# Moving a residual from GpSimd to VectorE slices, and reordering four places around the output projections

## The reference

```python
for i in range(2):
    x = layer_norm(ALPHA * x + 0.5 * swiglu(x, ffn1_w_gate[i], ffn1_w_up[i], ffn1_w_down[i]), ln_g[i, 0], ln_b[i, 0])
    proj = x @ (rwkv_w_in if i == 0 else sb_w_in)
    mix = rwkv7_mix(...) if i == 0 else stick_breaking_mix(...)
    heads = concatenate([mix, memory_attention(mq, mem_k, mem_v)])
    x = layer_norm(ALPHA * x + heads @ w_out[i], ln_g[i, 1], ln_b[i, 1])
    x = layer_norm(ALPHA * x + 0.5 * swiglu(x, ffn2_w_gate[i], ffn2_w_up[i], ffn2_w_down[i]), ln_g[i, 2], ln_b[i, 2])
```

## Time and profile before

| | |
|---|---|
| median of 3 runs | 1634.25 us (1630.9 to 1635.93) |
| the profiled execution | 1636.34 us |
| its span, first to last instruction | 1634.6 us |
| TensorE busy, mean granted clock | 1460.2 us (89%), 0.942 |
| VectorE / ScalarE / GpSimd busy | 958.9 / 675.2 / 231.0 us |
| DMA moved | 257.71 MB, mean 158 GB/s |

### The profile page before, as it was taken

One profiled execution on the slowest core, in us unless ns is written; L12 is line 12 of the kernel. 1 busy time (PEld: TensorE's weight loads), 2 busy tenths in 40 slices (PEclk: granted clock), 3 DMA queues, 4 the chain that ended last, 5 costly groups with the idle time before them and its releaser, 6 DMA issues. The chain is left out here.

```text
span 1634.6 us, 30766 instructions
## 1 busy us (share of the span) xinstructions
PE 1460.2 (89%) x12484; PEld 1328.6 (81%) x12484; DVE 958.9 (59%) x1213; ACT 675.2 (41%) x848; POOL 231.0 (14%) x208
## 2 busy tenths in 40 slices
PE   5999799997999978939867999979999895799997
PEld 4777699996999968828856999969999794589997
DVE  2665576666555565674538555585555547475556
ACT  4445455444333345542324333343334445343332
POOL 1440132220000024002303000030000302030000
PEclk8999999998999989969978999989999897789999
DMA  9954466663666644300024666656665440366662
GB/s 362 345 178 186 129 204 190 190 181 106 192 192 180 181 137 143 114 1 4 4 77 130 193 185 187 180 149 185 182 191 168 155 155 1 103 202 180 182 188 95
DMA packets 297827, 257.71 MB, mean 158 GB/s; under 512 B 6928, under 2 KB 274192, under 8 KB 294672
## 3 DMA queue, kind: packets, MB, share of 16 engines
q1 hardware_dynamic: 297744, 256.49, 50.7%
HBM read 255.42 MB, written 1.05 MB: 157 GB/s over the span
## 5 line engine op out<-in xcount | busy, mean ns | idle before, releaser
L137 PE MATMUL ps<-actT,a_parts 128*128 128x256 f32 x2176 | 626.3, 288 | 22.0 <-DVE actT L399 10.4
L138 PE MATMUL ps<-actT,a_parts 128*128 128x256 f32 x2176 | 622.5, 286 | 0.0
L139 PE MATMUL ps<-actT,a_parts 128*128 128x256 f32 x2176 | 622.2, 286 | 0.0
L137 PEld LDWEIGHTS ps<-actT,a_parts 128*128 128x128 f32 x2176 | 424.4, 195 | 33.4 <-issue 18.4
L138 PEld LDWEIGHTS ps<-actT,a_parts 128*128 128x128 f32 x2176 | 424.6, 195 | 3.6
L139 PEld LDWEIGHTS ps<-actT,a_parts 128*128 128x128 f32 x2176 | 424.4, 195 | 0.0
L1111 DVE TENSOR_TENSOR a_parts<-a_raw,a_parts 128x2048 fp32r<-128x2048 f32 x100 | 239.7, 2397 | 72.9 <-ACT a_parts L1108 72.7
L1108 ACT ACTIVATE a_parts<-a_raw 128x2048 fp32r<-128x2048 f32 x100 | 190.0, 1900 | 0.0
L1125 DVE TENSOR_TENSOR b_parts<-b_raw,b_parts 128x1024 fp32r<-128x1024 f32 x72 | 88.3, 1226 | 154.3 <-ACT b_parts L1122 154.3
L1122 ACT ACTIVATE b_parts<-b_raw 128x1024 fp32r<-128x1024 f32 x90 | 95.1, 1057 | 175.8 <-PE ps L139 175.8
L137 PE MATMUL ps<-b_parts,hid 128*128 128x512 f32 x400 | 157.8, 394 | 6.3 <-DVE hid L1192 6.3
(11 more groups left out here) (343 smaller groups left out, 1801.0 us busy)
## 6 DMA issues: line engine op xcount, KB each, us to landing
a_raw<-in_ffn_w_gate SPq DMA_DIRECT2D x88, 512.0 KB, 3.9
a_raw<-in_ffn_w_up SPq DMA_DIRECT2D x88, 512.0 KB, 5.1
b_raw<-in_ffn_w_down SPq DMA_DIRECT2D x88, 512.0 KB, 3.2
arena<-in_mod_w SPq DMA_DIRECT2D x24, 1024.0 KB, 8.9
a_raw<-in_f_up_w SPq DMA_DIRECT2D x44, 512.0 KB, 4.9
b_raw<-in_f_down_w SPq DMA_DIRECT2D x22, 512.0 KB, 3.2
a_raw<-in_rwkv_w_in SPq DMA_DIRECT2D x10, 1024.0 KB, 5.2
a_raw<-in_sb_w_in SPq DMA_DIRECT2D x10, 1024.0 KB, 5.4
```

Source lines behind the costliest of these rows:

```text
L137: pe.matmul(out, lhs[0], rhs[0], start=start, stop=False)
L138: pe.matmul(out, lhs[0], rhs[1], start=False, stop=False)
L139: return pe.matmul(out, lhs[1], rhs[0], start=False, stop=stop)
```

## The change

- GpSimd's residual is gone. In the feed-forward stages with a residual, VectorE does it inside the loop: nine iterations, each with one slice of 114 columns of both token halves, multiplied between the two halves of the iteration and added at its end. `x_tok` and `rows` are two columns wider for this (9 x 114 = 1026).
- For the rwkv and stick stages the residual moves behind them, into the output projection: VectorE does half 0 before the split of chunk 2 and half 1 before that of chunk 3, four passes of 1024 columns in all; SyncE loads the two rows there ahead of the chunks.
- Output projection on TensorE: chunk 2 for three blocks, then chunk 3 for these, then the last block, with half 0 turned in between. Before: block by block, both chunks each.
- rwkv: the small weights are loaded behind chunk 4 instead of ahead of everything.
- First block: the parameter table is loaded in two parts; chunk 1 of the second pointwise product (`g_pw2 + 1`) is split earlier on ScalarE and VectorE.
- Convolutional feed-forward: the split of the next stage's first chunk moves behind the first half's update.

```diff
+             ("mod_sh_m", D, mod(0)), ("mod_sc_m", D, mod(1)),
              ("norm_pre_ffn", D, whole("norm_pre_ffn")), ("a_pw1_b", 2 * D, whole("a_pw1_b")),
              ("a_dw_b", D, whole("a_dw_b")), ("a_ln_g", D, whole("a_ln_g")), ("a_ln_b", D, whole("a_ln_b")),
-             ("mod_sh_m", D, mod(0)), ("mod_sc_m", D, mod(1)), ("mod_sh_f", D, mod(3)), ("mod_sc_f", D, mod(4)),
...
-        x_tok = sb("x_tok", [P, NT, D])
+        x_all = sb("x_tok", [P, NT, D + 2])
+        x_tok = x_all[:, :, 0:D]
...
-        rows = sb("rows", [P, 2, D])
+        rows_all = sb("rows", [P, 2, D + 2])
+        rows = rows_all[:, :, 0:D]
...
-        def residual(pool, i, scale_row, offset_row):
-
-            pool.wait_ge(token_turned[1], 2 * i + 2)
-            for t in range(NT):
-                pool_steps.step(pool, pool.tensor_tensor(x_tok[:, t], x_tok[:, t], scale_row, ALU.mult))
-                ins = pool.tensor_tensor(x_tok[:, t], x_tok[:, t], offset_row, ALU.add)
-            ins.then_inc(pool_out.up("xs"), 1)
...
-                    sp.dma_start(x_tok[:], A["x"][0].rearrange("(t p) d -> p t d", p=P)).then_inc(x_loaded, 16)
-                    sp.dma_start(par[:], A["par"]).then_inc(params_loaded, 16)
+                    sp.dma_start(x_tok, A["x"][0].rearrange("(t p) d -> p t d", p=P)).then_inc(x_loaded, 16)
+                    sp.dma_start(par[:, 0:n_first], A["par"][:, 0:n_first]).then_inc(params_loaded, 16)
...
                     ring_a.load(sp, g_pw1 + 1)
+                    sp.dma_start(par[:, n_first:], A["par"][:, n_first:]).then_inc(rest_loaded, 16)
...
+                        if q == 2:
+                            ring_a.split_hi(act, g_pw2 + 1)
...
-                    for c in range(1, 4):
+                    for c in range(2, 4):
...
+                    ring_a.split_lo(dve, g_pw2 + 1)
...
+        RES_STEP = 114
...
-                        sp.wait_ge(pool_out.sem, pool_out.at("xs"))
+                        sp.wait_ge(res_done, r0 + BODY - 2)
...
-                        if got_norm is not None:
-                            pool.wait_ge(rows_loaded, rows_at)
-                            residual(pool, got, rows[:, 0], rows[:, 1])
...
+                    def residual(op, slot, j):
+                        w = bass.ds(j * RES_STEP + -RES_STEP, RES_STEP)
+                        row = rows_all[:, slot, w].unsqueeze(1).to_broadcast([P, NT, RES_STEP])
+                        return dve.tensor_tensor(x_all[:, :, w], x_all[:, :, w], row, op)
+
                     def tiles_dve(j):
                         split_a(None, dve, 0, j)
                         tile_dve(dve, 1, j - 1)
                         if not conv:
                             split_b(None, dve, 0, j)
+                        if got_norm is not None:
+                            residual(ALU.mult, 0, j).then_inc(res_scaled, 1)
                         split_a(None, dve, 1, j)
                         tile_dve(dve, 0, j)
                         if not conv:
                             split_b(None, dve, 1, j)
-
+                        if got_norm is not None:
+                            dve.wait_ge(res_scaled, j + r0)
+                            residual(ALU.add, 1, j).then_inc(res_done, 1)
+
+                    if got_norm is not None:
+                        dve.wait_ge(rows_loaded, rows_at)
                     with dve.Fori(1, BODY - 1) as j:
                         tiles_dve(j)
                     split_a(None, dve, 0, BODY - 1)
...
-                        ring_a.split_lo(dve, next_a)
-                    if conv:
...
                         updated(0)
+                        ring_a.split_lo(dve, next_a)
                         gated_y(1)
                         updated(1)
...
+                    load_row(sp, 0, norm_row("g", got_norm))
+                    load_row(sp, 1, norm_row("b", got_norm))
                     for g in range(g0 + 2, g0 + 4 + 2):
                         ring_a.load(sp, g)
...
+                    def residual(t):
+                        dve_steps.step(dve, dve.tensor_tensor(x_tok[:, t], x_tok[:, t], rows[:, 0], ALU.mult))
+                        dve_steps.mark(dve.tensor_tensor(x_tok[:, t], x_tok[:, t], rows[:, 1], ALU.add))
+
+                    dve.wait_ge(rows_loaded, rows_at)
+                    residual(0)
                     for c in range(2, 5):
+                        if c == 3:
+                            residual(1)
                         dve.wait_ge(ring_a.hi_done, g0 + c + 1)
                         dve.tensor_tensor(parts_of(c, 1), a_raw[:, (g0 + c) % 2], parts_of(c, 0).bitcast(F32),
                                           ALU.subtract).then_inc(ring_a.lo_done, 1)
+                    dve.wait_ge(dve_steps.sem, dve_steps.n)
                     norm_dve_side(dve, hand, yb, 1.0, norm, (ring_a.used, g0 + 4))
...
-                    for t, n in BLOCKS:
-                        for c in range(2, 4):
-                            if t == 0 and n == 0:
-                                ring_a.wait_split(pe, g0 + c)
-                            if t == 1 and n == 1 and c == 3:
-                                turn_tokens(pe, hand, 0)
-                            ins = down_chunk(pe, parts_of, c, t, n)
-                            if (t, n) == BLOCKS[3]:
-                                ins.then_inc(ring_a.used, 1)
-                        if (t, n) != BLOCKS[3]:
-                            ins.then_inc(acc_done, 1)
+                    ring_a.wait_split(pe, g0 + 2)
+                    for t, n in BLOCKS[:3]:
+                        down_chunk(pe, parts_of, 2, t, n)
+                    ring_a.wait_split(pe, g0 + 3)
+                    for t, n in BLOCKS[:3]:
+                        down_chunk(pe, parts_of, 3, t, n).then_inc(acc_done, 1)
+                    down_chunk(pe, parts_of, 2, *BLOCKS[3]).then_inc(ring_a.used, 1)
+                    turn_tokens(pe, hand, 0)
+                    down_chunk(pe, parts_of, 3, *BLOCKS[3]).then_inc(ring_a.used, 1)
...
-            norm_rows = [arena[:, used + r * D:used + (r + 1) * D] for r in range(2)]
-            pool_out.events(["xs"])
             with nc.Block() as block:
                 @block.sync
                 def _(sp):
-                    sp.dma_start(lora[0:HD], A["rwkv_w_up_2"][0]).then_inc(lora_loaded, 16)
-                    sp.dma_start(lora[HD:P], A["rwkv_a_up_2"][0]).then_inc(lora_loaded, 16)
-                    sp.dma_start(g_up, A["rwkv_g_up_2"][0]).then_inc(lora_loaded, 16)
-                    for r, which in enumerate("gb"):
-                        sp.dma_start(norm_rows[r], norm_row(which, take[3]).partition_broadcast(P)).then_inc(lora_loaded, 16)
                     for g in range(g0 + 2, g0 + 12 + 2):
                         ring_a.load(sp, g)
+                        if g == g0 + 4:
+                            sp.dma_start(lora[0:HD], A["rwkv_w_up_2"][0]).then_inc(lora_loaded, 16)
+                            sp.dma_start(lora[HD:P], A["rwkv_a_up_2"][0]).then_inc(lora_loaded, 16)
+                            sp.dma_start(g_up, A["rwkv_g_up_2"][0]).then_inc(lora_loaded, 16)
...
-                    pool.wait_ge(lora_loaded, 80)
-                    residual(pool, got, norm_rows[0], norm_rows[1])
...
-                                pe.wait_ge(lora_loaded, 80)
+                                pe.wait_ge(lora_loaded, 48)
...
-                    load_row(sp, 0, norm_row("g", take[3]))
-                    load_row(sp, 1, norm_row("b", take[3]))
```

More of the change, by code:

```diff
@@ L658, in _ @@
                     pool_steps.step(pool, pool.memset(ones_mean, 1.0 / D))
+                    pool_steps.step(pool, pool.memset(x_all[:, :, D:], 0.0))
+                    pool_steps.step(pool, pool.memset(rows_all[:, :, D:], 0.0))
                     pool_steps.step(pool, pool.memset(head_ones[:], 0.0))
@@ L662, in _ @@
                     constants_at.append(pool_steps.n)
-                    pool.wait_ge(params_loaded, 16)
+                    pool.wait_ge(rest_loaded, 16)
                     for j in range(KD):
@@ L1028, in build_program @@
         gated, scaled_x, root_ready = sem("gated"), sem("scaled_x"), sem("root_ready")
-        done = {"h": 0, "f_step": 0, "conv": 0, "gated": 0}
+        done = {"h": 0, "f_step": 0, "conv": 0, "gated": 0, "residual": 0}
+        res_scaled, res_done = sem("res_scaled"), sem("res_done")
+        RES_STEP = 114
         def ffn_stage(name, conv, norm, hand, next_a, next_b, take):
@@ L1054, in ffn_stage @@
             own_rows_at = rows_count[0]
-            if got_norm is not None:
-                pool_out.events(["xs"])
+            r0 = done["residual"]
+            done["residual"] += BODY - 2 if got_norm is not None else 0
             def b_of(q, j):
@@ L2470, in build_program @@
         rwkv_stages(take)
-        take = output_stage(0, 2)
+        take = output_stage(0, 2, 0)
         take = ffn_stage(("ffn2", 0), False, 2, 3, sec["ffn1", 1], sec[("ffn1", 1), "B"], take)
```

(2 more changed lines are left out.)

21 lines of the change are left out of this document (11 added, 10 removed).

## The result

The changed kernel takes 1609.05 us (median of 4 runs, 1607.90 to 1613.03) against 1635.01 us before: ratio 0.985, interval 0.9833 to 0.9866, so -24.5 us by the ratio and -26.0 by the medians. The forecast was 1621 with -13.0 and a range from 1613. The profiled execution took 1607.9 us, span 1606.2, mean granted clock 0.945.

A forecast was written before the change was run, and what follows sets the result against it. TensorE, busy 188.79 of 190 us in a feed-forward loop, was taken as the bound, with gains only at seams between stages. Terms -6.3 - 6.1 - 2.2 - 1.3 - 0.6 + 3.5 = -13.0 us gave 1621 us, range 1613 to 1628.

The forecast's parts named there:

- the unit for what follows: Feed-forward loop: some 8.5 us a half iteration, 0.12 us per 256-column matmul and 0.23 per 512, used to price the terms.
- 1, residual off GpSimd, -6.3: Feed-forward seams: without GpSimd's residual, VectorE's splits end sooner and TensorE's 6.3 us of waits for hid all go.
- rival D: Feed-forward loop: VectorE's residual slices stretch the loop, making the kernel slower than before, 1640 us; chance 0.04.
- 2, rwkv, -6.1: Start of rwkv: loading chunk 2 first removes a 3.72 us stall (-3.7) and the clock loss after it (-2.4).
- The clock term of -2.4: Start of rwkv: the granted clock no longer falls over 610 to 620 us once the stall is gone, -2.4 us.
- Rival E: Start of rwkv: GpSimd's earlier masks hold up VectorE's token splits by 1.5 us, giving 1622.5 us; chance 0.05.
- 3, first block, -4.1: First block: earlier chunk 1 split saves -2.2 of stall and -1.3 of clock, later parameters -0.6.
- the parameters: First block: taking 343 KB of parameters from the head of the DMA queue saves 0.6 us, bounds 0 and -2.
- 4, output stages, +3.5: Both output stages: the 3.03 us stall goes, but rows ahead of weights delay token half 0; +1.3 to +6.1, taken +3.5.
- The rows' term: Output stages: two row loads ahead of the weights cost 4.0 us of DMA, so chunk 2 lands that much later.
- The clock term: Output stages: TensorE's idle halves the clock, doubling transposes and six matmuls; first stage +3.5 instead of +1.1, second +2.6 instead of +0.2.
- rival A: Output stages: the rows delay no output weight, -5.1 in place of +3.5, giving 1613 us; chance 0.10.

The follow-up runs named there:

- e6: The changed kernel with the gates where x_tok was and widened x_tok behind hid, so TensorE's operands stand where they did before the change: 1624.64 us.
- e1: The kernel before with only x_tok and rows widened by two columns (rwkv masks' view of rows rewritten to fit): -18.1 us by the ratio, 0.9889.
- e12: The changed kernel with the residual of the three feed-forward stages back on GpSimd in whole passes, no slices on VectorE: 1617.88 us.
- e4: The changed kernel with the rwkv stage's five small loads issued ahead of its weight chunks again: 5.9 us more by the ratios.
- e8: The changed kernel with the first block's split of chunk 1 behind the last activation slice again, as before the change: 1609.55 us.
- e7: The changed kernel with output-stage row loads behind the first weight load, and chunk 2 split ahead of the residual's first half: 1608.49 us.

## Why the prediction was half right

**The step that failed** is the first: "the unit for what follows", 8.5 us a half iteration, "0.12 us for 256 columns and 0.23 for 512". These were taken as constants, and the wider tensors as free. They were a product of the layout: 119.9 and 228.8 ns at a distance of 65,536 bytes, 116.9 and 233.2 at 32 more. It is worth -13.4 us by e6 against the result, -12.5 by the counts, and no rival named it.

**The sum of the instructions came near, in part by luck**: forecast -13.0, measured -11.1 (-15.4 to -6.9) with the operands in their old places (e6), and -6.4 in the new layout (changed kernel against e1). One term failed outright and others missed the other way. Its terms by stages, e6 against before, one execution each. Stages with nothing to gain moved as well (rwkv core by -2.8, the convolutional feed-forward by +1.6), so a term is known to 2 us or so:

- **1, residual off GpSimd, -6.3:** right in mechanism, and the size lies between the two measurements: the three stages give -2.7 - 4.3 - 1.7 = -8.6 (unrounded), e12 in the new layout 4.7. Slices cost nothing in the loop; rival D did not occur, and the last stage's rows were no wait.
- **2, rwkv, -6.1:** right for the stall (3.72 to 0.18), too large for the clock. The stage gives -4.2, e4 4.7. The clock term of -2.4 brought 0.7 in e6 (4.2 less the 3.5 of stall) and 1.9 in e4 (4.7 less 2.8): the stretch at half clock that followed the stall is gone and the clock stands at 1.00 from 600 to 620 us, but the seam itself now stands at 0.53 (the third number from the end in the row below), as it does in e1 without the change's instructions (0.53 from 587 to 598). Rival E: no wait of the turned copy beyond 2.36 us (2.23 before); not seen.

```profile
589.00:600.00 11.00, 7.67 (x32) 6.83 (x32) 7.85 (x14) 4.48 (x8) 8.87 (x16) 0.53 0.30 95
```

- **3, first block, -4.1:** failed. The three parts sum to -0.2. The 1.24 us stall went, but the clock stood at half ahead of it for as much (e8), so that chunk 1's matmuls ended at 167.5 and not at 165.5, and chunk 3's high part waits for their end. The forecast had taken chunk 0 at full clock. The half clock behind chunk 3 is gone, but the one at 156 us, which costs 1.7 us, stands there instead, and the one at the block's end grew from 3.4 to 10.2 us (from 189.8). For the parameters 0.2 us of the 0.6 were seen, but e1, which still loads them in one part, reaches the first projection another 0.9 us sooner, so this term is not shown.
- **4, output stages, +3.5:** the sign depends on the layout: +2.0 in e6, -1.6 in the changed kernel against e1. The rows' term was too dear, as ScalarE's timeline of the changed kernel shows:

```profile
841.08 1.92 ACT L1532 ACTIVATE b_parts<-a_raw 128x2048 fp32r<-128x2048 f32 x1 [10.75 <-DMA a_raw<-in_w_out]
```

Chunk 2's high part starts 841.08 - 832.65 = 8.4 us into the stage, before 849.37 - 843.16 = 6.2 (843.16 was the stage's first matmul before): 2.2 us later and not 4.0, and e7 takes 1.7 of it back. The second block sum (856.62, in VectorE's rows at the top) starts 24.0 us in, as against 24.2 before and 25.6 forecast. The clock term came in one layout and not in the other. In the changed kernel TensorE's 2.57 us of idle time ahead of token half 0 did not lower the clock, and the transposes took 1.09 us. In e6 the idle time was 3.53 us and they took 1.97, the forecast's "twice as long", with the clock at 0.51 from 863 to 880.5; in its second output stage they took 1.57:

```profile
864.84 1.97 PE L371 MATMUL ps<-ident,x_tok 128*128 128x128 f32 x8 [3.53 <-DVE x_tok L351]
```

The place of the loss was right in both (a wait for token half 0 in place of the 3.03 us stall), rival A ("the rows delay nothing") was not.

The forecast's own tests told these apart: VectorE's splits, hid and the rwkv chunk came as written; chunk 3 of the first block came 0.3 us sooner and not 3.

## What to carry to other kernels

Any edit that changes the size or order of on-chip tensors can change the pace of matmuls that it doesn't touch, by 2.5% here; so time the new layout alone before crediting instructions (and expect that the two shares depend on which is taken first), and try a few small gaps (the study's best kernel is the changed one with a gap of 32 bytes and x_tok and the gates swapped, 1603.1 us). A duration per matmul read from one trace is a property of that layout. The whole gain from a removed stall can be missing where the clock stands at half in the same stretch (first block): price stalls by themselves, and the clock around them as a range that includes nothing.

## What the hardware showed that was not expected

- Start-to-start time of float32 matmuls of 256 columns with 128-column weight loads, by distance between the two operands' tensors over 65,536 bytes: 0: 119.9 ns; 32: 116.9; 64: 117.5; 96: 119.9; 128: 118.7; 160: 117.7. For 512 columns, b_parts and hid alone (distance over 40,960): 0: 229.0 to 229.5; 32: 233.1; 64: 233.4; 128: 231.3. Moving all tensors together does nothing (ratio 1.0004).
- The pace hardly depends on whether VectorE, ScalarE and GpSimd are busy (120.0 ns idle against 119.9 busy before, 117.2 against 116.7 after) or DMA transfers run.
- GpSimd passes over 1024 float32 with two SBUF inputs stretch two VectorE splits from 2.35 to 6.37 us in the new layout (e12) and to 6.75 in the old.
- An idle time of TensorE of 2.57 us (changed kernel, until 859.49) was followed by transposes at full clock (1.09 us), one of 3.53 us (e6, until 864.84) by the same at half clock (1.97 us), while in the changed kernel 3.4 us at half clock began at 156 us in a stretch in which TensorE was busy throughout.
